# A streaming encoder layer on one core: value products in two column halves, row sums taken from the exponentials

## What is computed

```python
s = einsum('bqhd,bkhd->bhqk', qn, k_nope) + einsum('bqhr,bkr->bhqk', qr, k_rope)
s = where(visible, s * scale, -inf)
p = softmax(s, axis=-1)
attn = einsum('bhqk,bkhd->bqhd', p, v)
mixed = sigmoid(gate_a) * attn + sigmoid(gate_b) * rec
x = x + mixed @ w_out
```

## Time and profile before

| | us |
|---|---|
| median of 3 runs | 876.79 (874.54 to 877.03) |
| profiled execution, its time | 874.96 |
| profiled execution, its span | 872.9 |
| PE busy in the span | 849.6 |
| DVE busy | 568.0 |
| ACT busy | 366.7 |
| POOL busy | 191.6 |

### The profile page before, as it was taken

How to read it: one execution, slowest core, us unless ns; L and a number is a source line. 1 busy time by engine, 2 the same in 40 slices (tenths; PEclk the granted TensorE clock), 3 DMA queues, 4 the chain that set the end, 5 groups by cost and what they waited for, 6 DMA issues and landing times.

```text
span 872.9 us, 16689 instructions
## 1 busy us (share of the span) xinstructions
PE 849.6 (97%) x6522; PEld 815.3 (93%) x6522; DVE 568.0 (65%) x998; ACT 366.7 (42%) x609; POOL 191.6 (22%) x206
## 2 busy tenths in 40 slices
PE   5999998899999999999999999999999999999998
PEld 5999998789999889877999999999999999999998
DVE  4586678767675676887656888778777876222121
ACT  6634959655655456657245221222222221122121
POOL 4021122202021121121140333323333234010000
PEclk9999999999999999999999999999999999999999
DMA  8433312031120101100223233232322323233321
GB/s 245 116 90 103 95 49 62 2 80 38 28 52 25 53 25 29 50 1 26 73 75 95 75 94 96 72 96 73 95 82 86 91 71 92 82 105 99 104 56 39
DMA packets 114466, 63.73 MB, mean 73 GB/s; under 512 B 7660, under 2 KB 112878, under 8 KB 114412
## 3 DMA queue, kind: packets, MB, share of 16 engines
q1 hardware_dynamic: 112428, 59.25, 23.7%
q0 software_dynamic: 1936, 3.70, 1.7%
q10 hardware_dynamic: 48, 0.02, 0.0%
HBM read 59.85 MB, written 2.70 MB: 72 GB/s over the span
## 4 chain that ended last, share of the span: by engine, by line
PE 87%; ACT 5%; DVE 4%; issue 2%; DMA 1%; SPq 0%; POOL 0%; ACTq 0%; DVEq 0%; POOLq 0%
PE PS L1605 49%; PE PS L1751 9%; PE PS L1833 6%; PE PS L1767 4%; PE PS L1805 4%; PE PS L1644 3%; PE PS L1710 2%; PE PS L2037 2%; PE PS L1787 2%; PE PS L1742 2%; PE PS L1706 1%; DMA xnat<-in_x_prompt_dram 1%; PE PS L1732 1%; PE PS L1673 1%; PE PS L1812 1%
## 5 line engine op out<-in xcount | busy, mean ns | idle before, releaser
L663 ACT ACTIVATE w_hi<-w_raw 128x1024 fp32r<-128x1024 f32 (+2 forms) x102 | 105.4, 1033 | 315.8 <-PE PS L1605 301.5
L1095 DVE TENSOR_TENSOR w_lo<-w_raw,w_hi 128x1024 fp32r<-128x1024 f32 (+2 forms) x102 | 124.7, 1223 | 117.7 <-ACT w_hi L663 117.5
L1605 PE MATMUL PS<-x2h,w_hi 128*128 128x274 f32 x704 | 147.7, 291 | 0.0
L1605 PE MATMUL PS<-x2h,w_lo 128*128 128x274 f32 x704 | 147.1, 290 | 0.0
L1605 PE MATMUL PS<-x2l,w_hi 128*128 128x274 f32 x704 | 147.1, 290 | 0.0
L1605 PEld LDWEIGHTS PS<-x2l,w_hi 128*128 128x128 f32 x704 | 112.1, 189 | 0.0
L1605 PEld LDWEIGHTS PS<-x2h,w_hi 128*128 128x128 f32 x704 | 112.0, 190 | 0.1
L1605 PEld LDWEIGHTS PS<-x2h,w_lo 128*128 128x128 f32 x704 | 111.4, 189 | 0.0
L625 POOL TENSOR_TENSOR uct<-uct 128x548 f32<-128x548 f32 x22 | 30.1, 1370 | 176.4 <-DVE uct L1558 176.4
L1605 PE MATMUL PS<-hh,w_hi 128*128 128x274 f32 x308 | 64.7, 292 | 0.0
L1605 PE MATMUL PS<-hh,w_lo 128*128 128x274 f32 x308 | 64.6, 291 | 0.0
(11 more groups left out here) (291 smaller groups left out, 1846.3 us busy)
## 6 DMA issues: line engine op xcount, KB each, us to landing
w_raw<-in_w_up_dram SPq DMA_DIRECT2D x44, 512.0 KB, 3.8
w_raw<-in_w_in_dram SPq DMA_DIRECT2D x24, 512.0 KB, 3.8
w_raw<-in_w_down_dram SPq DMA_DIRECT2D x16, 512.0 KB, 4.3
w_raw<-in_w_out_dram SPq DMA_DIRECT2D x8, 512.0 KB, 4.3
w_raw<-in_w_down_dram SPq DMA_DIRECT2D x8, 384.0 KB, 3.9
xnat<-in_x_prompt_dram SPq DMA_DIRECT2D x4, 512.0 KB, 5.2
w_raw<-in_w_in_dram SPq DMA_DIRECT2D x4, 416.0 KB, 7.6
wq<-in_w_q_b_dram SPq DMA_DIRECT2D x8, 192.0 KB, 2.5
```

The source lines that it names most:

```text
L663: nc.scalar.activation(hi[:, slot % 2, 0:n], raw[:, slot % 4, 0:n], ACT.Copy).then_inc(s_hi, 1)
L1095: tt(lo[:, slot % 2, 0:n], raw[:, slot % 4, 0:n], hi[:, slot % 2, 0:n].bitcast(F32), ALU.subtract).then_inc(s_lo, 1)
L1605: last = mm(PS[:, 2 * rank + j, 0:HT], w[:, slot % 2, cols], x[:, k0 + k, j * HT:(j + 1) * HT], start=(k0 + k == 0 and first), stop=(k0 + ...
```

## The change

The two heads take turns: tile n is block n // 2 of head n % 2, so widths go 128, 128, 256, 256, 384, 384, 512, 512. `values(p, t)` runs once for both heads, in steps 2, 4, 6 and 8, as products of 64 columns: head 0 writes rows 0 to 63 of bank 3 and head 1 rows 64 to 127. The exponentials give their row sums by `accum_out`; DVE inverts two of them at a time (`inverse_of_sums`, steps 1, 3, 5 and 7), and in `values` one product per head of 64 columns, whose weights are the inverse sums and whose moving operand is the identity, spreads them over bank 5. `gated_values` runs once for both heads, on 128 rows, in step 0 of the next pair, and multiplies by bank 5 as well. `head_sums` and `sums_inverse` go. The sample's sums are inverted apart, in `gated_sample`.

```diff
         def width(n):
-            return (n % 4 + 1) * P if n < 8 else HP + DEC
+            return (n // 2 + 1) * P if n < 8 else HP + DEC
...
             def mix(p):
-                pool.wait_ge(s_o, 3 * p + 3)
+                pool.wait_ge(s_ov, p + 1)
                 pool.wait_ge(s_ri, p + 1)
-                step.on(nc.gpsimd.tensor_tensor(o_p, o_p, sums[:, :], ALU.mult))
+                step.on(nc.gpsimd.tensor_tensor(o_p[:, S0:], o_p[:, S0:], sums[:, :], ALU.mult))
...
             def exps(p, n):
-                    nc.scalar.activation(Pn[:, n % 3, 0:w], bank[:, 0:w], ACT.Exp, bias=sm[:, 2:3]).then_inc(s_e, 1)
+                    nc.scalar.activation(Pn[:, n % 3, 0:w], bank[:, 0:w], ACT.Exp, bias=sm[:, 2:3],
+                                         accum_out=exp_sums(p, n)).then_inc(s_e, 1)
...
             def probs_columns(p, n):
                 if p or n >= 2:
-                    act.wait_ge(s_pv, p * 9 + n - 1)
+                    act.wait_ge(s_pv, p * 5 + (n // 2 if n > 1 else n - 1))
-            def head_sums(p, h):
...
+            def inverse_of_sums(p, t):
+                dve.wait_ge(s_e, 9 * p + 2 * t + 2)
+                c0 = 8 * (p % 2) + 2 * t
+                nc.vector.reciprocal(small[:, 7, 16 + c0:18 + c0], small[:, 7, c0:c0 + 2]).then_inc(s_r, 1)
-            def gated_values(p, h):
-                g_p = gate("A", p)[rows(h), 0:SEQ]
+            def gated_values(p):
+                g_p = gate("A", p)[:, 0:SEQ]
                 dve.wait_ge(s_gt, gate_count("A", p))
-                dve.wait_ge(s_pv, 9 * p + 4 * (h + 1))
-                stt(g_p, g_p, 1.0, values_bank(h)[rows(h), :], ALU.add, ALU.mult).then_inc(s_o, 1)
+                dve.wait_ge(s_pv, 5 * p + 4)
+                link(stt(g_p, g_p, 1.0, PS[:, 3, :], ALU.add, ALU.mult))
+                tt(g_p, g_p, PS[:, 5, :], ALU.mult).then_inc(s_ov, 1)
...
             def attend(p):
                 for n in range(9):
+                    if n % 2 and n < 8 and n + p > 1:
+                        inverse_of_sums(p, n // 2)
                     if n < 7:
                         row_max(p, n + 2)
...
                     if n == 0 and p:
                         gated_sample(p - 1)
+                        gated_values(p - 1)
...
             def scores(p, n):
-                h, t = divmod(n, 4)
+                t, h = divmod(n, 2)
...
+            def values(p, t):
+                par = p % 2
+                pe.wait_ge(s_ptf, p * 9 + (2 * t + 2))
+                if t == 0:
+                    pe.wait_ge(s_vf, p * 3 + 3)
+                    if p:
+                        pe.wait_ge(s_ov, p)
+                pe.wait_ge(s_r, 4 * p + t + 1)
+                for a in range(t + 1):
+                    for h in range(2):
+                        mm(PS[rows(h), 3, t * P:(t + 1) * P], V[:, par, a, 2 * h, :], PT[:, (h + p) % 2, a * P:(a + 1) * P],
+                           start=(a == 0), stop=(a == t))
+                for h in range(2):
+                    last = mm(PS[rows(h), 5, t * P:(t + 1) * P], inverse_sums(p, 2 * t + h).to_broadcast([P, VD]), ident[:, :],
+                              start=True, stop=True)
+                last.then_inc(s_pv, 1)
...
             def attend(p):
-                    if n:
-                        values(p, n - 1)
+                    if n and n % 2 == 0:
+                        values(p, n // 2 - 1)
```

More of the change, by code:

```diff
@@ L182, in layer @@
         xnl = fixed("xnl", [P, KD, T], F32R)
-        sums = fixed("sums", [P, T])
+        sums = fixed("sums", [P, DEC])
         zone = place
@@ L360, in width, with exp_sums, inverse_sums @@
         def width(n):
-            return (n % 4 + 1) * P if n < 8 else HP + DEC
+            return (n // 2 + 1) * P if n < 8 else HP + DEC
+        def exp_sums(p, n):
+            c0 = 8 * (p % 2) + n
+            return small[:, 7, c0:c0 + 1]
+        def inverse_sums(p, n):
+            c0 = 16 + 8 * (p % 2) + n
+            return small[:, 7, c0:c0 + 1]
         SP0 = 2 * P + R2
@@ L882, in probs_columns @@
                 nc.scalar.activation(PT[:, b, 0:w], PS[:, 6 + b, 0:w], ACT.Copy).then_inc(s_ptf, 1)
-            def head_sums(p, h):
[L886 to L889, removed]
             def sample_parts(p):
                 b = p % 2
-                act.wait_ge(s_pv, 9 * p + 9)
+                act.wait_ge(s_pv, 5 * p + 5)
                 nc.scalar.activation(PT[:, b, SP0:SP0 + P], PS[:, 6 + b, SP0:SP0 + P], ACT.Copy).then_inc(s_es, 1)
@@ L1328, in gated_sample @@
                     stt(g_p, g_p, 1.0, bank[rows(h), :], ALU.add, ALU.mult)
-                    last = nc.vector.tensor_copy(sums[rows(h), S0:], bank[rows(1 - h), :])
-                last.then_inc(s_o, 1)
+                    last = nc.vector.tensor_copy(sums[rows(h), :], bank[rows(1 - h), :])
+                last.then_inc(s_os, 1)
+                dve.wait_ge(s_os, p + 1)
+                nc.vector.reciprocal(sums[:, :], sums[:, :]).then_inc(s_ri, 1)
             def gated_recurrence(p):
@@ L1783, in transpose_probs @@
                 if n == 1 and p:
-                    pe.wait_ge(s_o, 3 * p)
+                    pe.wait_ge(s_os, p)
                 bank = PS[:, 6 + (n + p) % 2, :]
-                for a in range(n % 4 + 1 if n < 8 else 2):
+                for a in range(n // 2 + 1 if n < 8 else 2):
                     last = nc.tensor.transpose(bank[:, a * P:(a + 1) * P], Pn[:, n % 3, a * P:(a + 1) * P], ident[:, :])
@@ L1790, in transpose_probs @@
                 last.then_inc(s_pt, 1)
[L1792 to L1796, removed]
-                    pe.wait_ge(s_vf, p * 3 + 3)
-                if n == 0 and p < 2:
-                    pe.wait_ge(s_clear, p + 1)
[L1800 to L1809, removed]
-                            tile, h = 4 + a + 2 * (g // 2) if a < 2 else NKT - 1, g % 2
-                            c0 = a * P + g * DEC
-                            last = mm(PS[g * DEC:(g + 1) * DEC, 6 + b, SP0:SP0 + P], PT[:, b, c0:c0 + DEC],
-                                      V[:, par, tile, h:h + 2, :].rearrange("p h n -> p (h n)"),
-                                      start=(a == 0), stop=(a == (1 if g >= 2 else 2)))
@@ new lines, in sample_parts @@
+            def sample_parts(p):
+                par, b = p % 2, p % 2
+                pe.wait_ge(s_ptf, p * 9 + 9)
+                if p < 2:
+                    pe.wait_ge(s_clear, p + 1)
+                for a in range(3):
+                    for g in range(4 if a < 2 else 2):
+                        tile, h = 4 + a + 2 * (g // 2) if a < 2 else NKT - 1, g % 2
+                        c0 = a * P + g * DEC
+                        last = mm(PS[g * DEC:(g + 1) * DEC, 6 + b, SP0:SP0 + P], PT[:, b, c0:c0 + DEC],
+                                  V[:, par, tile, h:h + 2, :].rearrange("p h n -> p (h n)"),
+                                  start=(a == 0), stop=(a == (1 if g >= 2 else 2)))
@@ L1912, in attend @@
                         values_in(p + 1, u, (u + 1) % 2)
-                values(p, 8)
+                sample_parts(p)
             def early_keys(g):
```

47 lines of the change are left out of this document (15 added, 32 removed).

## The result

The changed kernel took 882.33 us (median of 5 runs, 879.24 to 882.93) against 876.11 for the kernel before on the same chip: ratio 1.0066, 95% interval 1.0054 to 1.0078. The forecast was 879.7 us, slower. The profiled execution of the changed kernel is one of the slowest of the five, 882.93 us with a span of 880.9, so that it stands 8.0 above the profiled one of before.

A forecast was written before the change was run, and what follows sets the result against it. PE's chain was taken to bound full pairs, with DVE and ACT waits in pairs 0, 5, 6 and 7. Terms 1.2 + 1.84 + 1.1 - 0.2 + 0.8 = +4.7 on 874.96 gave 879.7 us, range 870.7 to 886.

The forecast's parts named there:

- Value products: PE's value and spread products in each pair: 28 sets of two halves side by side, 3.08 us instead of 4.46.
- Rival (c): Column halves run side by side but each set waits for its weight load: 1.5 us a pair, 892 us; chance 0.06.
- Trips: PE entering and leaving column halves, four new trips a pair: 0.34, 0.34, 0.30 and 0.14 us, sum 1.12.
- The wait ahead of the gate product: PE, arriving 1.0 us earlier, waits 0.74 us for DVE's key columns before a pair's first gate product.
- (b): Rival: no wait ahead of the gate product, DVE and ACT being quicker; pairs 0 to 5 regain 0.74 each, 875.3; chance 0.25.
- Full pairs: Pairs 1 to 4: -0.27 us up to the gate product and +0.73 behind it, +0.46 each, 1.84 together.
- Pairs 0 and 5: Pair 0: about +0.5 us at DVE's chain and +0.73 behind, +1.2; pair 5, where PE waits for ACT: +1.1.
- Pair 6: DVE's reciprocals go, but ACT's chain sets a later row nearly alone: -0.2 us (between -1.0 and +0.3).
- Pair 7 and the tail: Gated products ahead of a row maximum, last mixed column 0.6 later: +0.8 us (0 to +1.5); at the end nothing.
- (d): Rival: more waits in pairs 5 to 7 through accumulator reads, 16 steps of 0.2, 883 us; chance 0.49 with the forecast.
- The clock: PE's clock is granted in full in every slice, so no part of the forecast rests on it.

The follow-up runs named there:

- run 1: Changed kernel without the second head's values, each pair of 64-column products made one of 128 columns, so no changes into or out of column halves: 875.08 us, 0.9994.
- run 6: Changed kernel, block 0's value group run with block 1's in step 4, DVE's gated values moved behind the key columns in step 3: 880.34 us, 1.0040.
- run 2: Changed kernel with, in pairs 0 to 5, the score product of tile 6 put ahead of the first gate product: 877.17 us, 1.0015.
- run 4: Changed kernel; pairs 5 and 6: ACT's value-projection copy, tanh, first mixed column behind the sample exponentials; pair 7: output split in step 3: 880.94 us, 1.0057.
- run 5: Changed kernel without row sums from the exponentials, the table of sums set to one once at the start: 881.59 us, 1.0055.
- run 10: Changed kernel with each group's value products written head by head instead of taking turns: 886.05 us, 1.0122.

## Why the prediction was right

The direction, the distance of 36.2 and most terms held; the total came 2.6 us above the forecast. Part of the closeness is luck, as the list shows. Step by step:

- **Value products.** 28 sets of 0.11, as counted. The sentence of the Trainium skill, "TensorE: Matmul & The Clock Gate", Part 3, "The mechanism", by which a load overlaps a product only when the row groups differ, would have spread the sets: the trace disagrees. The same section of the Trainium skill also lets a load into the background weights go ahead of products in flight, and the trace doesn't speak against that. Rival (c) falls.
- **Trips.** Counted 1.12 a pair, measured 0.9 (run 1). The ways out cost 0.20, 0.19, 0.13 and 0.18, near the 0.19 of the earlier trace rows, into the gate product too (3.24 against 3.05). The two ways in that can be seen cost 0.14 each. The first way in is missing, 0.34 counted for a trip that cost 0.2: the group starts behind a wait of 0.11 and takes 0.44 with a change of columns (the changed kernel) as without one (0.46 in run 1). The profile names no cause for that wait, but by the times it ends with DVE's inverse of the row sums: L1317 ends at 275.73, the group's loads start at 275.85, and the second group, whose inverses are long done, doesn't wait. It is the only place in the chain of a full pair where DVE's list, and not the turn-around of a bank, seems to hold PE up. The Trainium skill, "TensorEngine Tiling (Array Packing)", "Key Properties", says that changing the mode drains the engine, without a price; the price at each change agrees with that, though no row shows a drain as such.
- **The wait ahead of the gate product.** Counted 0.74, measured 0.64 in the loads' row. The place was right; the size came out near by luck, as the cause was wrong. The prediction blamed DVE's longer list, which it had finishing as late as before, with PE merely earlier. The rows above and run 6 show DVE with time to spare. What uncovered the turn-around (transposes into a bank, a copy out of it, a product into it) was PE's order: before, three value products (0.67) stood between the key transposes and the gate product; in the new order nothing does. Run 2 fills the gap and gets 0.7 back. (b) falls.
- **Full pairs.** By the chain's starts, the part from the sample's products to the next gate product fell by 12.15 - 11.71 = 0.44 (counted 0.27), the part behind rose by 24.49 - 23.66 = 0.83 (counted 0.73): +0.39 against +0.46.
- **Pairs 0 and 5**, stretch by stretch: to pair 0's gate product +0.51 (counted 0.5), from there to pair 1's +0.31 (0.73 - 0.27 = 0.46), from pair 5's gate product to its sample +1.42 (0.61 + 0.44 + 0.21 + 0.14 = 1.40): tenths.
- **Pair 6.** Counted -0.2 (between -1.0 and +0.3), came out +0.60 in the profiled execution. The clock is the reason, and it is not in the sum at all. In run 2 the list of pair 6 is the same and the wait for ACT's list is the same 1.78, but the clock held: 25.64, 0.8 shorter than before. So the clock at half level took 1.4 here, and without it the count was in its range.
- **Pair 7 and the tail.** Mis-sized: +0.8 (0 to +1.5) counted, 1.85 + 0.37 measured; 0.17 of it is the end of the low clock (20.40 in run 2). Against run 2, run 4 took back 0.57 there, with the split of an output tile moved, and run 6 0.52, with DVE's gated values moved and a trip less; the prediction had named both and counted 0.6 and 0.35 for them. The rest wasn't traced to one cause. (d) is no part of it (run 5).
- **The clock.** The prediction took it as full in every slice, from a row of nines, and left it out. It was full in the attention pairs before, but 0.96 in the first 40 us. Of the 8.0 between the profiled executions 1.29 lie ahead of attention, where only the clock was found to differ, and 1.6 in pairs 6 and 7 are the clock's. That leaves 5.1 against the 4.7 of the sum: pairs 0 to 5 came 0.25 lower than counted, pair 6 0.6 lower, pair 7 and the tail 1.25 higher.

What stays open is how much of the 6.2 us between the medians is the clock. Of the five executions three list a mean granted clock of 0.990 (882.93, 882.91, 882.33), the others 0.994 (881.11) and 0.996 (879.24); none of the 57 executions of the kernel before beside the experiments lists less than 0.992. At a listed 0.996 those have a median of 874.55, at 0.994 one of 875.40, so at like clocks the changed kernel is 4.7 and 5.7 slower. These are single executions of it, and no run set the clock by itself.

## What to carry to other kernels

- Work that stands between a transpose and the product that writes the same bank again is cover, even where the profile shows no wait. When an edit moves it away, price the whole turn-around (here 0.7 us a pair); then look for other ready work to put there.
- Column halves that run side by side save passes, but each entry and exit costs some 0.1 to 0.2 us. Batch groups so that there are few trips: with three instead of four, the gap filled, and the order of pairs 6 and 7 changed, the change became a gain of 0.45%.
- A 9 in a row of tenths is not full. Before leaving the clock out of a sum, read it by windows, in several executions.
- The same edit can be right in steps with cover and wrong in the last ones without (gated values in pair 6, ACT's order in pair 5). Read the end pieces apart.

## What the runs showed of the hardware

- In pair 6 PE's loads stood still for 1.78 us in an otherwise busy stretch; some 1.7 us after that its clock was granted at half for about 3.4 us, and ten projections took 2.21 us instead of 1.19. Run 5 shows the same. In runs 1, 2 and 6 an equal wait (1.78 at 388.90, 389.33 and 395.25) had no such stretch behind it, so the wait alone doesn't decide it.
- Products of different column halves can start in another order than they are written (run 10). The first group is written alike in both kernels; of the others the second, of 8 records, costs nothing when written head by head (0.59 as in the changed kernel), the third, of 12, costs 0.26 and the fourth, of 16, 0.49.
- A DVE operation with two operands in SBUF seems to be held by POOL; one row shows it, and no run tested it. A mixed column that takes 0.71 to 0.73 in the seven other cases took 1.82 in the changed kernel, while POOL added for 1.36; first DVE's timeline, then POOL's:

```profile
405.21 1.82 DVE L1351 SCALAR_TENSOR_TENSOR mxl<-U,mxh 128x548 fp32r<-128x548 f32 x1
```

```profile
405.08 1.36 POOL L577 TENSOR_TENSOR U<-U,gates 128x548 f32<-128x548 f32 x1
```
